# Seven block products for each pair of gate columns, with the convolution's norm moved into the attention slots

## The chip, the cores and the metric

The kernel runs on one core of a Trainium2 chip. The metric is the time of one execution in device microseconds, the median of several runs.

## What is computed

One encoder layer over 1024 positions of width 1024. What matters here is the first half, the mixing of positions:

```python
proj = x @ w_in[l] + b_in[l]
glu_in, q, k, v, gate_logits = jnp.split(proj, splits, axis=-1)     # 1024 | 512 | 512 | 512 | 2048 columns
y_conv = conv_branch(glu_in, ...)      # a * sigmoid(gate), 31 taps per channel, LayerNorm over 512 channels, SiLU, product
y_attn = chunked_attention(heads(q), heads(k), heads(v), rel_bias[l]) @ w_attn_out[l]
g_conv, g_attn = jnp.split(jax.nn.sigmoid(gate_logits), N_BRANCHES, axis=-1)
mixed = (g_conv * y_conv + g_attn * y_attn) @ w_o[l] + b_o[l]
x = layer_norm(ALPHA * x + mixed, ln1_g[l], ln1_b[l])
x = layer_norm(ALPHA * x + grouped_moe(x, ...), ln2_g[l], ln2_b[l])
```

Everything is float32. The expert half (16 experts, 2 used by each position) follows and is not touched, except for names of semaphores.

## The kernel before

Each product is made of float32r parts: ACT copies an operand into a rounded "high" tile, DVE (or POOL) subtracts it from the original into a "low" tile, and PE adds high x high, high x low and low x high (`mm3`, L544 to L546). A weight block is 128 columns of a weight matrix with all 1024 rows, 512 KB. SP loads block n into one of four ring slots once the slot's last block has been used (`wait_used`), ACT makes `wh` (L863), DVE makes `wl` (L1025).

A whole block is 8 row chunks x 2 halves of the sequence x 3 matmuls of 128x512, 48 in all. The order of PE is written by hand:

1. Blocks 0 to 7 are the convolution's input (values and gates). After each pair ACT takes the sigmoid and DVE makes `u` (`glu`, L1039).
2. Blocks 8 to 23 are the 16 gate blocks (`gate_job`). ACT writes their sigmoids to `gst`, and SP stores them to memory for later.
3. Meanwhile DVE does the convolution: 4 channel groups x 31 taps (`conv_tap`, L1052, first taps L1049), 7 taps per block. PE sums over channels with a matrix of ones (`conv_mean` before gate 14, `conv_var` before gate 15). DVE subtracts the mean (L1083), adds squares (L1066), takes one reciprocal of 128x1024 (L1089), and normalises (L1094); ACT applies SiLU (L920) while PE works on the first query and key blocks.
4. Eight tiles of v (128x256 matmuls), then the first query and key blocks in four half sums.
5. Attention in 32 slots (4 head pairs x 8 tiles of 128 queries). In slot n, PE makes the scores (L616), part of the next pair's query/key block, the weighted values of slot n-2 (L644) and the transposes of slot n-1 (L630). DVE takes the maxima of slot n (L1144), reciprocals (L1153), sums (L1163, L1168) and low parts of transposed tiles (L1175). ACT takes exponentials (L931), and POOL scales them (L499).

The DVE order in a slot before:

```python
for n in range(LATE):
    maxima(n)
    if n >= 2:
        transposed_lo(n - 2, now_and_late(n - 2)[1])
    inverse_sums(n)
    ...
    for p in qk_ended(n):
        qk_low(p, ps[:, qk_bank(p), :])
    if n >= 2:
        values_sum(n - 2)
    if n >= 1:
        transposed_lo(n - 1, now_and_late(n - 1)[0])
```

Of the kernel before, what the change touches and what calls it, by code (L numbers as in the profile page):

```python
# [13 lines left out]
P = 128  # L14
# [24 lines left out]
TAPS_A_STEP = 7  # L39
DMA_SCRATCH = 8192  # L40
# [5 lines left out]
B_GATE = 2 * CB  # L46
B_V = (24, 32)
B_Q = (26, 28, 30, 34)
B_OC, B_OA, B_WO = 36, 40, 44
N_BLOCKS = 52  # L50
LAST_GATES = (14, 15)


def block_columns():

    a, g, q, k, v, gate = 0, 4, 8, 12, 16, 20
    cols = []
# [26 lines left out]
def encoder_layer(nc, xT, x, wblk, b_in, dw, dwb, lncg, lncb, relb, b_o, ln1_g, ln1_b,  # L84
                  w_r, b_r, wexp, ln2_g, ln2_b, consts, out):
    x1_dram = nc.dram_tensor("x1_rows", (1 + SEQ, D), F32, kind="Internal").ap()
    acc_dram = nc.dram_tensor("acc_rows", (SEQ + P, D + 1), F32, kind="Internal").ap()
    gate_dram = nc.dram_tensor("gate_cols", (N_GATE, P, SEQ), F32, kind="Internal").ap()
    ctx = ExitStack()
    with ctx:  # L90
# [19 lines left out]
        csum = at("csum", [P, SEQ], F32, 112)  # L110
        sqr = at("sqr", [P, CB, SEQ], F32, 128)
# [83 lines left out]
        small = 211  # L195
# [24 lines left out]
        tab = tiny("tab", [P, 5, TAB], I32)  # L220
# [21 lines left out]
        par_in = sem("par_in"); bias_in = [sem(f"bias_in{i}") for i in range(2)]  # L242
# [7 lines left out]
        g_sig = sem("g_sig"); gs_out = [sem(f"gs_out{i}") for i in range(2)]  # L250
        mean_done = sem("mean_done"); cent = sem("cent"); sq_done = sem("sq_done"); sum_ok = sem("sum_ok")
        var_done = sem("var_done"); std_done = sem("std_done"); rstd_ok = sem("rstd_ok")
# [12 lines left out]
        row_in = [sem(f"row_in{i}") for i in range(TT)]  # L265
        lnp_in = sem("lnp_in"); xres_ok = sem("xres_ok")
# [5 lines left out]
        def wait_used(eng, n):  # L272

            if n < B_V[0]:
                eng.wait_ge(blk_used, n + 1)
            elif n in B_V or n - 1 in B_V:
# [9 lines left out]
        def place(n):  # L286

            if B_WO <= n < B_WO + 4:
                i = n - B_WO
                return wh2[:, i], wl2[:, i], raw2[:, i], raw2_in[i], 16  # L290
            s = n % RING
            return wh[:, s], wl[:, s], raw[:, s], raw_in[s], 16 * ((n if n < B_WO else n - 4) // RING + 1)

# [52 lines left out]
        SPLITS = {1: (30,), 2: (31,), 5: (32,), 9: (33,), 13: (34,), 17: (35,), 25: (36,), 27: (37,), 29: (38,), 30: (39,),  # L346
                  31: (40,), 32: (41,), 33: (42,)}
# [39 lines left out]
        def gate_q(g):  # L387

            return g if g < LAST_GATES[0] else 15 + 2 * (g - LAST_GATES[0])

        moe_parts = moe(nc, sem, locals())

        with nc.Block() as block:
            @block.sync
            def _(sp):
# [1810 lines left out]
```

## Time and profile before

| What | Value |
|---|---|
| median of 3 runs | 1134.77 us (1133.7 to 1134.91) |
| span of the profiled execution | 1130.7 us |
| median of the runs over that span | 4.07 us |
| busy: PE, DVE, ACT, POOL | 97%, 71%, 47%, 20% |
| chain that ended last, share of PE | 85% |
| mean granted TensorE clock | 0.991 |

The profile gives the span of its execution and not a separate device time for it; the 4.07 us between the span and the median of the runs is taken as what lies around a span. Busy shares are averages over stages. A matmul's listed duration overlaps the next one, so its rate is read from a window: time over count.

### The profile page before, as it was taken

To read this page: it belongs to the slowest core of one execution; us is meant where nothing else is said; L and a number is where in the kernel's file an instruction comes from. 1 tells how busy PE (TensorE), PEld (TensorE's weight loads), DVE (VectorE), ACT (ScalarE), POOL (GpSimd) and SP (SyncE) were. 2 spreads that over 40 slices of the span, in tenths; PEclk is the share of its full clock that TensorE was granted. 3 is DMA by queue.
4 is the path that set the end of the run, shared out by engine and by line. 5 is a ranking of instruction groups with operands and counts; after the bars stand their busy time and mean duration, and the time that the engine had idled before them with its cause. 6 is when DMAs were issued, how large, how long until landed. Compare 5 with 4: busy or idle time off the path is not lost.

```text
span 1130.7 us, 17012 instructions
## 1 busy us (share of the span) xinstructions
PE 1098.3 (97%) x5583; PEld 913.1 (81%) x5584; DVE 803.2 (71%) x1152; ACT 529.2 (47%) x787; POOL 227.4 (20%) x190
## 2 busy tenths in 40 slices
PE   8999999999999999999999999999999999999984
PEld 7888888888978789878888888787888888888762
DVE  5799999935447766666685588888679556558866
ACT  5111111123456665645331134467578545557755
POOL 0000000000046864757100000013121211212110
PEclk9999999999999999999999999999999999999998
DMA  7121233232111010181632325889999876699966
GB/s 266 56 84 56 83 104 104 83 112 93 57 38 43 19 43 1 65 326 39 251 118 88 142 119 196 278 331 354 324 331 381 311 230 192 236 352 341 368 177 269
DMA packets 49800, 199.58 MB, mean 177 GB/s; under 512 B 7249, under 2 KB 7633, under 8 KB 47682
## 3 DMA queue, kind: packets, MB, share of 16 engines
q1 hardware_dynamic: 43538, 176.19, 41.9%
q0 software_dynamic: 6192, 22.49, 8.0%
q8 instruction: 40, 0.66, 0.2%
q14 instruction: 30, 0.25, 0.1%
HBM read 166.21 MB, written 32.52 MB: 176 GB/s over the span
## 4 chain that ended last, share of the span: by engine, by line
PE 85%; DVE 4%; DMA 4%; ACT 3%; POOL 2%; issue 2%; ACTq 0%; DVEq 0%; SPq 0%; POOLq 0%
PE ps L544 16%; PE ps L546 16%; PE ps L545 16%; PE ps L1570 9%; PE ps L1572 9%; PE ps L1571 9%; PE ps L644 2%; PE ps L630 2%; DMA gu<-in_wexp 2%; PE ps L616 2%; DMA dn_raw<-in_wexp 2%; PE ps L1651 1%; PE ps L1566 1%; POOL pr L499 1%; PE ps L1678 1%
## 5 line engine op out<-in xcount | busy, mean ns | idle before, releaser
L544 PE MATMUL ps<-xh,wh 128*128 128x512 f32 x512 | 203.3, 397 | 2.0 <-DVE xl L1030 1.7
L545 PE MATMUL ps<-xl,wh 128*128 128x512 f32 x512 | 199.5, 390 | 0.0
L546 PE MATMUL ps<-xh,wl 128*128 128x512 f32 x512 | 199.5, 390 | 0.0
L1469 DVE TENSOR_TENSOR gu<-gu (+1 forms) x128 | 148.6, 1220 | 33.6 <-issue 21.5
L499 POOL TENSOR_SCALAR pr<-pr,rinv 128x640 f32<-128x640 f32 (+4 forms) x64 | 95.4, 1503 | 379.7 <-DVE rinv L1153 379.5
L1052 DVE SCALAR_TENSOR_TENSOR cv<-u,dw_t,cv 128x1024 f32<-128x1024 f32 x120 | 154.1, 1284 | 3.7
L1570 PE MATMUL ps<-gu,xgh 128*128 x336 | 134.0, 399 | 4.0 <-DVE gu L1469 2.2
L1463 ACT ACTIVATE gu<-gu (+1 forms) x128 | 124.4, 1048 | 20.6 <-DMA gu<-in_wexp 13.0
L1572 PE MATMUL ps<-gu,xgl 128*128 x336 | 131.9, 393 | 0.0
L1571 PE MATMUL ps<-gu,xgh 128*128 x336 | 131.4, 391 | 0.0
L544 PEld LDWEIGHTS ps<-xh,wh 128*128 128x128 f32 x512 | 96.1, 188 | 25.4 <-issue 6.4
L546 PEld LDWEIGHTS ps<-xh,wl 128*128 128x128 f32 x512 | 96.1, 188 | 20.5
L545 PEld LDWEIGHTS ps<-xl,wh 128*128 128x128 f32 x512 | 96.2, 188 | 19.1 <-issue 0.5
L863 ACT ACTIVATE wh<-raw 128x1024 fp32r<-128x1024 f32 x52 | 54.6, 1058 | 98.3 <-DMA raw<-in_wblk 98.0
L1025 DVE TENSOR_TENSOR wl<-raw,wh 128x1024 fp32r<-128x1024 f32 x40 | 50.3, 1260 | 47.7 <-ACT wh L863 47.5
L1570 PEld LDWEIGHTS ps<-gu,xgh 128*128 128x128 f32 x336 | 63.5, 189 | 17.9 <-issue 5.3
L2063 DVE TENSOR_TENSOR dn_l<-dn_raw,dn_h 128x1024 fp32r<-128x1024 f32 x60 | 69.5, 1220 | 9.9 <-ACT dn_h L1811 9.8
L1572 PEld LDWEIGHTS ps<-gu,xgl 128*128 128x128 f32 x336 | 63.4, 189 | 13.6
L1571 PEld LDWEIGHTS ps<-gu,xgh 128*128 128x128 f32 x336 | 63.6, 189 | 12.7
L1570 PE MATMUL ps<-dn_h,hbh 128*128 128x512 f32 x168 | 67.7, 403 | 2.5 <-DVE hbl L2067 2.5
L1572 PE MATMUL ps<-dn_h,hbl 128*128 128x512 f32 x168 | 66.3, 394 | 0.0
L1571 PE MATMUL ps<-dn_l,hbh 128*128 128x512 f32 x168 | 66.1, 394 | 0.0
(278 smaller groups left out, 2022.4 us busy)
## 6 DMA issues: line engine op xcount, KB each, us to landing
gu<-in_wexp SPq DMA_DIRECT2D x64, 1024.0 KB, 9.1
dn_raw<-in_wexp SPq DMA_DIRECT2D x16, 2048.0 KB, 9.8
raw<-in_wblk SPq DMA_DIRECT2D x52, 512.0 KB, 4.2
gate_cols<-gst SPq DMA_DIRECT2D x16, 512.0 KB, 5.3
xf<-acc_rows SPq DMA_DIRECT2D x8, 512.5 KB, 8.1
xraw<-in_xT SPq DMA_DIRECT2D x8, 512.0 KB, 7.3
gcm<-gate_cols SPq DMA_DIRECT2D x8, 512.0 KB, 7.5
gam<-gate_cols SPq DMA_DIRECT2D x8, 512.0 KB, 14.5
```

The lines of the kernel that those rows point to most:

```text
L499: pool.tensor_scalar(pr[n % 3][:, h, 0:nt * P], pr[n % 3][:, h, 0:nt * P], rinv[:, n % 3, h:h + 1], None, ALU.mult).then_inc(p_ready, 1)
L544: pe.matmul(o, a_h, b_h, start=first, stop=False)
L545: pe.matmul(o, a_h, b_l, start=False, stop=False)
L546: return pe.matmul(o, a_l, b_h, start=False, stop=last)
L863: act.activation(hi, src, ACT.Copy).then_inc(w_hi, 1)
L1052: dve.scalar_tensor_tensor(out=cv[:, j, :], in0=tap, scalar=w, in1=cv[:, j, :], op0=ALU.mult, op1=ALU.add).then_inc(conv_d, 1)
L1463: eng.activation(gu[:, par, k, 0, :], gu[:, par, k, 1, :].bitcast(F32), ACT.Copy).then_inc(gu_hi, 1)
L1469: eng.tensor_tensor(gu[:, par, k, 1, :], gu[:, par, k, 1, :].bitcast(F32), gu[:, par, k, 0, :], ALU.subtract).then_inc(gu_lo, 1)
L1570: pe.matmul(o, a_h, b_h, start=first, stop=False)
L1571: pe.matmul(o, a_h, b_l, start=False, stop=False)
L1572: return pe.matmul(o, a_l, b_h, start=False, stop=last)
L2063: dve.tensor_tensor(dn_l[:, k, :], dn_raw[:, k, :], dn_h[:, k, :], ALU.subtract).then_inc(dn_lo, 1)
```

## The change

The 16 gate blocks form 8 pairs. For a pair, the product of a 2x2 grid of weight parts (2 blocks x 2 halves of the rows) with a 2x2 grid of input parts (2 halves of the rows x 2 halves of the sequence) was 8 block products. It becomes 7, in the scheme with 4 sums of weights, 4 sums of inputs and 7 sums of results. A block product ("unit") is 4 chunks x 3 = 12 matmuls of 128x512, and there are 56.

- POOL makes the weight sums with DMAs from memory to memory: per pair 4 copies and 4 adding transfers of 256 KB, issued in 7 rounds of up to 16, each round waiting for all of the one before.
- SP loads 56 units of 256 KB into 8 slots, in place of 16 blocks. A summed unit waits for its round.
- DVE makes the four input sums (128x2048 each) and their low parts; ACT makes the high parts.
- For each unit ACT makes a high part, DVE a low part (128x512); DVE adds results (7 additions per pair), ACT copies one product and takes four sigmoids per pair.
- Each block of the first eight still has 7 taps beside it (from the third on), but in the gate stage one tap goes with each unit. Sixteen more stand beside the v tiles and ten behind them.
- The mean's matmuls stand between the third and fourth query/key half sums, the centring behind them; squares, variance, square root, reciprocal, normalisation and SiLU stand in attention slots 0 to 9.
- The two first bias tiles are scaled by POOL instead of DVE.
- v tiles use other PSUM banks, and the query/key sums wait for all eight low parts of v.

The core of the diff. Of the two functions named `conv_late` the first is ACT's, called ahead of a slot's exponentials, and the second DVE's, called between `maxima(n)` and the rest of slot n:

```diff
+UNIT_SLOTS = 8
+PARTS = {1: (0, 0), 2: (0, 1), 4: (1, 1)}
+SUMS = {5: 0, 6: 1, 7: 2, 3: 3}
+ORDER = (1, 6, 5, 7, 2, 3, 4)
+UNITS = [(x, q) for q in range(KC) for x in ORDER]
...
+                            if stage:
+                                pool.dma_start(o, a, accum_op=ALU.add, max_dma_last_dim=4096).then_inc(wsum_in, 16)
+                            else:
+                                pool.dma_start(o, a).then_inc(wsum_in, 16)
+                for r in range(KC // 2 + 3):
+                    if r:
+                        pool.wait_ge(wsum_in, 16 * sums_issued(r - 1))
+                    for stage in range(4):
+                        weight_sums(r - stage, stage)
...
+                def gate_product(m):
+                    x, q = UNITS[m]
+                    s, bank = m % UNIT_SLOTS, m % 8
+                    pe.wait_ge(u_lo, m + 1)
+                    if m < 8:
+                        pe.wait_ge(u_ready, CB - 1 + (m >= 4))
+                    else:
+                        bank_read(m - 8)
...
+                    for k in range(CB):
+                        last = mm3(ps[:, bank, :], uh[:, s, k], ul[:, s, k], b_h[:, k, :], b_l[:, k, :],
+                                   k == 0, k == CB - 1)
+                    last.then_inc(blk_used, 1)
...
-                    v_tile(0, t, ps[:, 4 + t % 4, 0:2 * P])
+                    v_tile(0, t, ps[:, V_BANKS[t % 4], 0:2 * P])
+                pe.wait_ge(v_lo, TT)
                 for i in range(2):
...
+                        if i and h == 0:
+                            conv_mean()
...
                 for n in range(LATE):
                     scores_of_slot(n)
+                    if n == VAR_SLOT:
+                        conv_var()
...
+                def conv_late(n):
+                    if n == 1:
+                        act.wait_ge(stat_done, 2)
+                        act.activation(std[:], psf[:, 6 * HALF:8 * HALF], ACT.Sqrt, scale=1.0 / DC, bias=eps[:]).then_inc(sq_done, 1)
+                    if n == SILU_SLOT:
+                        for j in range(CB):
+                            act.wait_ge(nrm, j + 5)
+                            act.activation(cv[:, j, :], cv[:, j, :], ACT.Silu, scale=cpar[:, 1, j:j + 1],
...
+                for m in range(N_UNITS):
+                    if m + 4 < N_UNITS:
+                        unit_low(m + 4)
+                    if m == 0:
+                        glu(CB - 1)
+                    if m:
+                        gate_sums(m - 1)
+                    some_taps(TAPS_A_PRODUCT)
...
                 for t in range(TT):
+                    some_taps(2)
+                    v_low(0, t, ps[:, V_BANKS[t % 4], 0:2 * P])
...
+                some_taps(CB * CW)
...
+                def conv_late(n):
+                    if n == 0:
+                        for j in range(1, CB):
+                            square_sum(j)
+                    if n in (2, 3):
+                        dve.wait_ge(sq_done, CB + 1)
+                        for i in range(2 * n - 4, 2 * n - 2):
+                            c = slice(2 * P * i, 2 * P * i + 2 * P)
+                            dve.reciprocal(rstdc[:, c], std[:, c]).then_inc(nrm, 1)
+                    if 4 <= n < 4 + CB:
+                        normalise(n - 4)
```

Three places in the instruction order, all on DVE. In the names, `cv` is the convolution's sum, `ul` and `uh` a unit's low and high part, `gst` the gate results, `vhl` the parts of v, `pr` the attention tile and `nmx` its maxima.

The gate stage before, in its middle:

```order
L1052 SCALAR_TENSOR_TENSOR cv<-u,dw_t,cv 128x1024 x7
L1025 TENSOR_TENSOR wl<-raw,wh 128x1024
L1052 SCALAR_TENSOR_TENSOR cv<-u,dw_t,cv 128x1024 x7
L1025 TENSOR_TENSOR wl<-raw,wh 128x1024
L1052 SCALAR_TENSOR_TENSOR cv<-u,dw_t,cv 128x1024 x7
```

And now:

```order
L1230 TENSOR_TENSOR ul<-uraw,uh 128x512
L1256 TENSOR_TENSOR gst<-ps,gst 128x512
L1212 SCALAR_TENSOR_TENSOR cv<-u,dw_t,cv 128x1024
L1230 TENSOR_TENSOR ul<-uraw,uh 128x512
L1212 SCALAR_TENSOR_TENSOR cv<-u,dw_t,cv 128x1024
L1230 TENSOR_TENSOR ul<-uraw,uh 128x512
L1256 TENSOR_TENSOR gst<-ps,gst 128x512
```

Seven taps and one 128x1024 subtraction per block of 48 matmuls became one tap, one 128x512 subtraction and on average one addition from PSUM per unit of 12.

The v stage before ends like this:

```order
L1099 TENSOR_TENSOR vhl<-ps,vhl 128x2x128 x4
L1113 TENSOR_SCALAR bias_75<-bias_75 128x1280
L1115 MEMSET bias_75 64x2x64
L1116 MEMSET bias_75 64x2x64
L1113 TENSOR_SCALAR bias_76<-bias_76 128x1280
L1115 MEMSET bias_76 64x2x64
```

And now, up to the first maxima:

```order
L1212 SCALAR_TENSOR_TENSOR cv<-u,dw_t,cv 128x1024 x2
L1324 TENSOR_TENSOR vhl<-ps,vhl 128x2x128
L1212 SCALAR_TENSOR_TENSOR cv<-u,dw_t,cv 128x1024 x2
L1324 TENSOR_TENSOR vhl<-ps,vhl 128x2x128
L1212 SCALAR_TENSOR_TENSOR cv<-u,dw_t,cv 128x1024 x10
L1220 TENSOR_TENSOR csum<-csum,cv 128x1024
L1332 SCALAR_TENSOR_TENSOR ql_77<-ps,b_in_t,qh_75 128x512 x2
L1348 SCALAR_TENSOR_TENSOR cv<-ps,cv 128x1024 x4
L1332 SCALAR_TENSOR_TENSOR kl_81<-ps,b_in_t,kh_79 128x512 x2
L1185 TENSOR_TENSOR wl<-raw,wh 128x1024 x2
L1384 ISA pr_86,nmx<-ps,bias_84 128x128
```

Taps stand ahead of each low part of v, and the last taps, the channel sum and the centring stand ahead of the key's low parts, which the first scores need.

Attention slot 2 on DVE before:

```order
L1144 ISA pr_79,nmx<-ps,bias_75 128x384
L1144 ISA nmx 128x1
L1153 RECIPROCAL rinv<-rs 128x1 x2
L1163 TENSOR_TENSOR attn<-ps,attn 64x128 x2
L1168 TENSOR_TENSOR attn<-ps,attn 64x128 x2
```

And now:

```order
L1384 ISA pr_88,nmx<-ps,bias_84 128x384
L1384 ISA nmx 128x1
L1364 RECIPROCAL rstdc<-std 128x256 x2
L1393 RECIPROCAL rinv<-rs 128x1 x2
L1403 TENSOR_TENSOR attn<-ps,attn 64x128 x2
L1408 TENSOR_TENSOR attn<-ps,attn 64x128 x2
L1415 TENSOR_TENSOR pthl<-ps,pthl 128x4x128
```

Half of the reciprocal over 1024 positions stands between the slot's maxima and everything else that PE waits for; slot 3 has the other half. Over the whole program PE's list shrinks from 5412 to 5316 rows.

## Rows read from the trace of the kernel before

**Rows 1.** Busy time by stretch, us: engine busy (instructions), granted clock, DMA share, GB/s.

```profile
core 0: us, PE busy (x) PEld busy (x) DVE busy (x) ACT busy (x) POOL busy (x), PEclk, DMA share, GB/s
95.80:247.80 152.00, 152.00 (x672) 125.88 (x671) 128.73 (x103) 30.26 (x28) 0.00 (x0) 1.00 0.30 90
272.94:295.97 23.03, 23.03 (x194) 23.03 (x192) 10.83 (x13) 4.75 (x9) 0.00 (x0) 1.00 0.22 70
295.97:317.85 21.88, 21.88 (x99) 17.85 (x98) 7.17 (x12) 10.16 (x11) 0.00 (x0) 1.00 0.22 72
317.85:339.93 22.08, 22.08 (x129) 17.52 (x128) 12.90 (x45) 15.10 (x35) 14.09 (x11) 1.00 0.17 48
339.93:364.65 24.72, 24.30 (x167) 20.78 (x166) 18.45 (x54) 16.75 (x40) 17.86 (x11) 1.00 0.15 49
```

**Rows 2.** Waits of PE up to 520 us: total, times, longest us.

```profile
PE ps L544 <- DVE xl L1030: 1.7, 1, 1.7
PE ps L630 <- POOL pr L499: 1.4, 2, 0.8
```

**Rows 3.** Groups of DVE up to 330 us: busy us, mean ns | idle before.

```profile
L1052 DVE SCALAR_TENSOR_TENSOR cv<-u,dw_t,cv 128x1024 f32<-128x1024 f32 x120 | 154.1, 1284 | 3.7
L1025 DVE TENSOR_TENSOR wl<-raw,wh 128x1024 fp32r<-128x1024 f32 x30 | 36.6, 1224 | 44.8 <-ACT wh L863 44.6
L1089 DVE RECIPROCAL rstdc<-std 128x1024 f32<-128x1024 f32 x1 | 6.6, 6553 | 1.2 <-ACT std L891 1.2
L1039 DVE SCALAR_TENSOR_TENSOR u<-ps,b_in_t,sig 128x1024 f32<-128x1024 f32 x4 | 5.1, 1278 | 0.0
L1066 DVE TENSOR_TENSOR sqr<-sqr 128x1024 f32<-128x1024 f32 x3 | 3.7, 1225 | 1.2 <-ACT sqr L888 1.0
L1099 DVE TENSOR_TENSOR vhl<-ps,vhl 128x256 fp32r<-128x256 f32 x8 | 3.4, 425 | 12.8 <-ACT vhl L903 12.8
```

**Rows 4.** Timeline of DVE, first blocks: start, duration us.

```profile
21.00 1.23 DVE L1025 TENSOR_TENSOR wl<-raw,wh 128x1024 fp32r<-128x1024 f32 x1 [0.24 <-ACT wh L863]
38.02 7.89 DVE L1052 SCALAR_TENSOR_TENSOR cv<-u,dw_t,cv 128x1024 f32<-128x1024 f32 x6
46.96 9.21 DVE L1052 SCALAR_TENSOR_TENSOR cv<-u,dw_t,cv 128x1024 f32<-128x1024 f32 x7
```

**Rows 5.** Timeline of PE: first product, mean, scores of slots 0 and 5, values in slot 9.

```profile
8.16 0.47 PE L544 MATMUL ps<-xh,wh 128*128 128x512 f32 x1 [1.71 <-DVE xl L1030]
247.64 1.88 PE L583 MATMUL ps<-csum,ones_c 128*128 128x512 f32 x4
317.85 0.33 PE L616 MATMUL ps<-kh,qh 64*128 64x128 f32 x2
339.93 0.41 PE L616 MATMUL ps<-kh,qh 64*128 64x320 f32 x2
368.83 1.36 PE L644 MATMUL ps<-pthl,vhl 128*128 128x256 f32 x10
```

**Rows 6.** Timeline of ACT at a table load, and the group of SiLUs.

```profile
296.17 0.38 ACT L903 ACTIVATE vhl<-ps 128x256 fp32r<-128x256 f32 x1 [2.50 <-PE ps L546]
296.57 1.28 ACT L920 ACT_TABLE_LOAD   x1
...
L920 ACT ACTIVATE cv<-cv,cpar 128x1024 f32<-128x1024 f32 x4 | 4.6, 1231 | 0.0
```

**Rows 7.** The first 15 us, columns as in rows 1.

```profile
0.00:15.00 15.00, 11.55 (x44) 9.32 (x46) 9.13 (x9) 10.13 (x11) 1.73 (x12) 1.00 0.88 345
```

**Rows 8.** POOL DMA issues, ns min/median/max; landing; packets of one scatter (791.6 to 803).

```profile
L1507 POOL DMA_INDIRECT acc_rows<-ys,to_now x20: 1591/1607/2427, 755.5 to 1089.7; - x20
...
L1497 POOL DMA_INDIRECT xg<-x_rows,id_now x19: 965/1006/1187, 731.2 to 1052.3; - x19
...
acc_rows<-ys,to_now POOLq DMA_INDIRECT x20, 9.3
...
q0 software_dynamic: 144, 0.52, 29.7%
```

More of the change, by code:

```diff
@@ L289, in place, with gate_weights, sum_round, sums_issued @@
                 i = n - B_WO
-                return wh2[:, i], wl2[:, i], raw2[:, i], raw2_in[i], 16
+                return wh2[:, i], wl2[:, i], raw2[:, i], raw2_in[i], 48 if i < 2 else 16
             s = n % RING
             return wh[:, s], wl[:, s], raw[:, s], raw_in[s], 16 * ((n if n < B_WO else n - 4) // RING + 1)
+        def gate_weights(q, n, k):
+            return wblk[W_GATE + 2 * q + n][:, CB * k:CB * k + CB, :]
+        def sum_round(x, q):
+            return q // 2 + {5: 1, 7: 1, 6: 2, 3: 3}[x]
+        def sums_issued(r):
+            return sum(2 * many for g in range(KC // 2) for stage, many in enumerate((4, 2, 1, 1)) if g + stage <= r)
+        U2, W, U3, C22, C11, C12, C21 = range(1, 8)
+        def sum_no(which, q):
+            return 7 * q + which
+        def sigmoids_at(m):
+            if not 0 <= m - 2 < N_UNITS:
+                return []
+            x, q = UNITS[m - 2]
+            return [(q, slot) for after, slot in ((7, 3), (2, 0), (3, 2), (4, 1)) if after == x]
+        SIGMOIDS = [x for m in range(N_UNITS + 2) for x in sigmoids_at(m)]
+        def sigmoid_no(q, slot):
+            return SIGMOIDS.index((q, slot)) + 1
+        V_BANKS = (0, 1, 2, 3)
         def tiles_of(c):
@@ L593, in v_part @@
+                    last.then_inc(stat_done, 1)
                 def v_part(s, t, o, ks):
@@ new lines, in _ @@
+                    if n == 0:
+                        for i in range(4):
+                            act.wait_ge(t_sum, i + 1)
+                            act.activation(t_high[i], t_raw[i], ACT.Copy).then_inc(x_hi, 1)
+                    j = n // 2
+                    if n % 2:
+                        act.wait_ge(blk_used, n + 1)
+                        if j >= 2:
+                            act.wait_ge(u_ready, j - 1)
+                        g = 4 * (j % 2) + 2
+                        act.activation(sig[:, j % 2, :], psf[:, HALF * g:HALF * g + SEQ], ACT.Sigmoid,
+                                       bias=b_in_t[:, CB + j:CB + j + 1]).then_inc(sig_ready, 1)
@@ L899, in v_high @@
+                for m in range(N_UNITS + 2):
+                    if m < N_UNITS:
+                        copy_product(m)
+                    if m + 4 < N_UNITS:
+                        unit_high(m + 4)
+                    elif m + 4 < N_UNITS + 2:
+                        high(B_V[0] + m + 4 - N_UNITS)
+                    for q, slot in sigmoids_at(m):
+                        gate_sigmoid(q, slot)
                 def v_high(s, t, o):
@@ L952, in _ @@
                 for i in range(2):
-                    act.wait_ge(gs_out[i], 16 * KC)
+                    for slot in range(4):
+                        act.wait_ge(row_moved[4 * i + slot], GATES_STORED)
                 def conv_high(n):
@@ new lines, in _ @@
+                assert taps == CB * CW
+                for i in range(2):
+                    qk_low(i, ps[:, i, :])
+                dve.wait_ge(stat_done, 1)
+                for j in range(CB):
+                    dve.scalar_tensor_tensor(out=cv[:, j, :], in0=psf[:, 4 * HALF:6 * HALF], scalar=-1.0 / DC, in1=cv[:, j, :],
+                                             op0=ALU.mult, op1=ALU.add).then_inc(cent, 1)
+                for i in range(2, 4):
+                    qk_low(i, ps[:, i, :])
@@ L1131, in maxima @@
+                for i in range(2):
+                    for slot in range(4):
+                        dve.wait_ge(row_moved[4 * i + slot], GATES_STORED)
                 def maxima(n):
```

425 lines of the change are left out of this document (254 added, 171 removed).

## The prediction

> **What bounds the kernel now.** I read busy time by stretch first. In the gate stage PE is busy in all of 152.0 us, for 672 matmuls, so one costs 152.0 / 672 = 0.226 us; a block of 48 takes 10.86 us and a unit of 12 will take 2.71 us. The granted clock is 1.00 there and in the stretches after it [rows 1]. PE's waits come next: in the first 520 us the longest are 1.7 us at the start and 1.4 us for POOL [rows 2]. So each matmul taken out before the experts is worth its full time, and each wait put in costs its full time, since nothing later on PE is idle enough to win it back. The reader should then look at DVE in the same stretches: 128.7 of 152.0, 10.8 of 23.0, 7.2 of 21.9, 12.9 of 22.1 and 18.5 of 24.7 us [rows 1]. That idle time must hold all that the change adds to DVE.
>
> **What is taken away.** PE's list has 96 rows fewer, all of them gate matmuls: 96 x 0.226 = **21.7 us**. The four matmuls of the mean (1.88 us with their overlap, about 1.7 in the queue [rows 5]) and the four of the variance are only moved.
>
> **What is put on the path.** Durations of DVE for sizes that the trace lacks come from the line through 256 columns (425 ns) and 1024 columns (1224 ns) [rows 3]: 0.69 us for 512 and 2.3 for 2048.
>
> (a) *Start.* POOL's first round copies 8 x 256 KB = 2.1 MB from about 2 us on, beside the loads of x, whose stretch runs at 345 GB/s [rows 7]; PE is paced by them, for it waits for the first low part of x and then has 0.6 us of slack. If none of it gets in the way this costs 0, if all goes first 2.1 MB / 345 GB/s = 6.1 us. I take 2, a third, since the copies are issued one by one, a plain one in about 1.0 us of POOL [rows 8].
>
> (b) *Unit 4 waits for `glu(3)`.* DVE is free at 22.2 us [rows 4]. It makes the four input sums (4 x 2.3, to 31.4), a `wl` behind ACT's rounded parts of them (to 35.6) and their four low parts (to 44.4). Then 6 x 7 taps at 9.2 us for seven [rows 4] less the two cheap first taps make 54.3, three `wl` 3.4, five unit low parts 3.1 and four `glu` 4.8 (1.2 each, back to back) [rows 3]: 110.0 us. PE could start unit 4 at 95.8 + 4 x 2.71 = 106.7. Cost 3.3; between 1 and 6, for 88 us of queue are added up. From there DVE needs about 17.5 us per seven units (7 x 0.6 low parts, 7 x 0.66 additions, 7 x 1.25 taps) against PE's 19.0, so it keeps ahead, with ACT at under half. This cover is thin: 0.2 us more per unit would use it up.
>
> (c) *v to query/key.* Between the last unit and the eighth low part of v, DVE has one addition 0.7, 16 taps 20.5, eight low parts 3.4 and two `wl` 2.4 [rows 3]: 27.0, or 26.7 with their overlap, against 23.0 us of PE [rows 1]. PE now waits for all eight: 3.7 (3 to 5).
>
> (d) *The way to the first scores.* From the start of the query/key sums (time 0) DVE has ten taps, the channel sum and two low parts, to 15.8. The mean's matmuls run from 16.3 to 18.0, the four centrings to 22.9; ACT squares the last until 24.1 and only then takes the key's high part (24.8), DVE its low part (25.5). Scores start at 25.6 where they stood at 21.9 [rows 1]; 1.7 of that is the mean. Cost 2.0 (1 to 4).
>
> (e) *Slots 0 to 4.* PE waits, followed in the queues: 1.3 for a `wl` that now stands behind (d); 2.5 for three square additions of 1.2 [rows 3] ahead of the variance; 0.8 because ACT loads the square root's table, takes the root and loads the exponential's table ahead of slot 1's exponentials; 2.1 and 3.5 for the two halves of the reciprocal, 3.3 us each (6.55 in one piece [rows 3]), which stand ahead of the inverse sums, the low parts and the next maxima. That is 10.2, of which 0.6 comes back: 9.6. Lower bound 5: DVE is busy 12.9 of 22.1 us there, so has 9.2 idle for 10.3 of new work [rows 1]. Upper 12.
>
> (f) *Slots 4 to 7*, one normalisation of 1.2 each against 6.3 us idle [rows 1]: 1.5 (0 to 4).
>
> (g) *SiLU in slot 9.* Ahead of that slot's exponentials ACT now has a table load, four SiLUs (4.6) and the load back: 1.28 + 4.6 + 1.28 = 7.2 us [rows 6]. The late transposed tile of slot 7 is queued behind it, and the weighted values, at 368.8 before [rows 5], wait for that tile. ACT had some 1.6 us idle there: 5.5 (2 to 7).
>
> Nothing else is charged: scaling two bias tiles on POOL (3.5 us each) lies in the 20 us before the first maxima, and everything behind slot 9 keeps its order.
>
> **Sum.** 2 + 3.3 + 3.7 + 2.0 + 9.6 + 1.5 + 5.5 = 27.6 put in, 21.7 taken out: **+5.9 us** on a span of 1130.7. The median of the runs is 4.07 above that span, so 1134.77 + 5.9 = **1140.7**. With all terms at their low ends (12) the result is -9.7, with all at the high ends (44) +22.
>
> A rule weighed against a row. A table load stands 0.02 us behind the operation before it and takes 1.28 us, after which SiLU starts at once [rows 6]. The Trainium skill (ScalarE: Activation LUTs, What ACT_TABLE_LOAD costs) adds a drain of 1.38 us to each switch. The row shows none, and decides; with it, four more switches in the slots would add up to 5.5 us and the time would be 1146.
>
> **Rivals.**
>
> *B, faster: the slots absorb it.* PE's queue in each early slot holds a filler of 12 matmuls (2.7 us), placed so that the chain from maxima to transposes has time; if the queues overlap better than I follow them, (e) and (g) shrink. With (a) at 0, (b) 2, (c) 3, (d) 1, (e) 5, (f) 0 and (g) 2 the sum is 13, and the time 1134.77 - 8.7 = 1126. It decides as soon as (e) and (g) together are under 6.9 us instead of 15.1. For it: PE waits almost nowhere today. Against: DVE's added 10.3 us in slots 0 to 3 exceed its idle time. Chance 0.27.
>
> *C, a draw*, within 2.3 us of the time before (0.2%, about what a measurement of this kernel can tell from no change): (e) and (g) near 9. Chance 0.15.
>
> *D, the weight sums come late.* Unit 5 is the first to need the fourth round, so 8 + 12 + 14 + 16 = 50 transfers with four landings between. With 32 copies at 1.0 us, 18 adding ones at 1.6 and 9.3 us to land [rows 8] that is 2 + 32 + 29 + 37 = 100 us, and the data is needed by about 106. At the longest issues seen, 1.19 and 2.43 us [rows 8], it is 121, which is 15 late: 1155; with all 50 at 2.43, 160 and about 1190. SP's queue waits in order, so later loads are late with it. Later rounds have slack: 144 packets of one scatter, 0.52 MB, took 29.7% of 11.4 us of the 16 engines, or 3.4 us [rows 8], and 32 such transfers of half the size need 54 us of some 200. Chance 0.11. The Trainium skill (SBUF — State Buffer, SBUF: two separate sides) says that POOL cannot write descriptors while DVE holds their shared port in its fast mode; by that, POOL's issues would stretch beside a busy DVE, and this rival is how it would show. No row shows the rule at work on plain transfers.
>
> That the change does not do what it says is excluded by PE's list.
>
> **How the numbers follow.** Forecast 0.47 at 1140.7, B 0.27, C 0.15, D 0.11. Faster by over 0.2%: 0.27; within: 0.15; slower: 0.47 + 0.11 = 0.58. The likeliest case's own range is 1137 to 1152. The range 1123 to 1160 leaves out about half of D and the thin ends of B and of the forecast.
>
> **What would show it.** Right: 56 units at 2.71 us; a wait of PE of about 3 us for `u` or `ul` near 107 us; about 4 us for `vhl` before the query/key sums, near 276; waits for `sqr` and for DVE's reciprocals in slots 1 to 4; a wait of about 5 us near 370 behind ACT's SiLU. Wrong: PE at over 99% through slots 0 to 9 (B), waits for unit loads behind POOL's rounds (D), or a unit stage longer than 160 us, which would mean that DVE's additions are dearer than 0.66 us.

## The result and the profile after

| | before | changed |
|---|---|---|
| median, us | 1134.24 (1132.82 to 1134.91, 4 runs) | 1159.8 (1155.37 to 1160.31, 4 runs) |
| ratio | 1 | 1.0217, 95% interval 1.0196 to 1.0238 |
| profiled execution: own time, span, us | 1134.77, 1130.7 | 1159.61, 1157.8 |
| granted clock, mean | 0.991 | 0.975 |

Slower was right, the size was not: +25.6 us where +5.9 was forecast. The time lies at the upper edge of the whole range (1123 to 1160) and above the likeliest case's own (1137 to 1152). The busy table of the changed kernel, cut where PE starts the first product, the first unit, the v tiles, the query/key sums and the scores of slots 0, 5, 9 and 11 (the columns are those of [rows 1]):

```profile
8.01:100.79 92.78, 88.64 (x385) 71.71 (x386) 76.99 (x57) 28.18 (x26) 32.33 (x50) 1.00 0.86 238
100.79:262.89 162.10, 154.87 (x673) 127.45 (x672) 150.99 (x181) 56.75 (x93) 7.16 (x9) 0.98 0.56 157
262.89:296.19 33.30, 23.45 (x194) 23.04 (x192) 33.02 (x31) 8.86 (x15) 8.01 (x6) 0.92 0.35 119
296.19:324.00 27.81, 26.13 (x102) 20.36 (x102) 20.67 (x19) 6.78 (x8) 0.00 (x0) 0.91 0.10 24
324.00:356.89 32.89, 28.51 (x132) 21.36 (x132) 25.59 (x56) 18.36 (x38) 14.57 (x11) 0.84 0.09 29
356.89:382.72 25.83, 24.29 (x167) 20.75 (x166) 22.03 (x56) 16.34 (x38) 17.35 (x11) 1.00 0.13 47
382.72:400.39 17.67, 12.45 (x57) 9.89 (x56) 7.14 (x25) 14.18 (x24) 6.80 (x6) 0.81 0.00 1
```

And the stretch of before that answers to the last line:

```profile
364.65:374.32 9.67, 9.37 (x58) 7.66 (x57) 7.01 (x24) 6.72 (x17) 3.59 (x3) 1.00 0.00 1
```

Against [rows 1] this gives the ledger of the span. The first unit starts 5.0 us later (100.79 for 95.80). The units take 162.1 us; 672 matmuls took 152.0 before, so 10.1 are lost there. The v tiles lose 10.3 (33.3 for 23.0). The query/key sums lose 4.2 beside the 1.7 of the moved mean, slots 0 to 4 lose 9.1 beside the 1.7 of the moved variance, slots 5 to 8 1.1, the stretch of slot 9 8.0, all the rest 1.0. That is 48.8 put in and 21.7 taken out: +27.1, the difference of the spans (1157.8 - 1130.7). PE's waits up to 420 us name the causes (the line left out is 1.7 us for POOL's `zeros` at the start, which the kernel before has too):

```profile
PE ps L651 <- DVE vhl L1324: 9.8, 2, 9.4
PE ps L769 <- DVE pthl L1415: 6.4, 3, 4.5
PE ps L651 <- DVE u L1199: 5.9, 1, 5.9
PE ps L651 <- DVE xl L1190: 4.1, 5, 1.2
PE ps L651 <- DVE ql L1332: 3.5, 2, 2.7
...
PE ps L741 <- DVE kl L1332: 1.7, 1, 1.7
PE ps L651 <- DVE ul L1230: 1.4, 1, 1.4
PE ps L651 <- DVE wl L1185: 1.2, 1, 1.2
```

These are 34 us, where [rows 2] had nothing over 1.7, and all eight are waits for DVE. They are not the whole loss. Five times PE's granted clock stands at a half (of its two levels, 1.2 GHz instead of 2.4) behind a wait. The same columns for these five stretches:

```profile
119.35:122.90 3.55, 3.55 (x9) 2.78 (x9) 3.55 (x5) 0.00 (x0) 0.35 (x1) 0.50 0.58 113
296.19:300.62 4.43, 4.43 (x10) 3.46 (x11) 4.32 (x4) 0.00 (x0) 0.00 (x0) 0.50 0.00 0
325.78:330.64 4.86, 4.86 (x11) 3.81 (x12) 4.65 (x8) 3.44 (x6) 0.00 (x0) 0.50 0.00 0
352.28:354.37 2.09, 2.09 (x6) 1.60 (x5) 2.09 (x7) 0.71 (x1) 0.89 (x1) 0.51 0.00 0
393.95:398.78 4.83, 4.83 (x12) 3.77 (x12) 2.63 (x11) 2.59 (x6) 3.90 (x3) 0.50 0.01 3
```

In them one matmul follows another after 0.427 us instead of 0.227, so 19.8 us of them cost about 19.8 x (1 - 0.227 / 0.427) = 9.3 us. This is an estimate and the least: right behind the five stretches another 4.7 us run at 0.51 to 0.53, which by the same sum would be 2.2 us more. The kernel before has a granted clock of 1.00 in each of the stretches of [rows 1].

### The profile page after: what moved, and what is told of

Its sections match the earlier page's. It is cut to its first block, busy times and chain, and to the rows that moved or that the text cites. A ratio compares the mean times of both kernels' runs of the same rounds, so it can differ in the third digit from the quotient of the medians.

```text
span 1157.8 us, 17221 instructions
## 1 busy us (share of the span) xinstructions
PE 1094.1 (94%) x5487; PEld 905.0 (78%) x5488; DVE 866.4 (75%) x1253; ACT 560.2 (48%) x856; POOL 282.5 (24%) x259
## 4 chain that ended last, share of the span: by engine, by line
PE 58%; DVE 10%; ACT 4%; DMA 4%; issue 2%; POOL 1%; ACTq 0%; DVEq 0%; SPq 0%; POOLq 0%
PE ps L1810 9%; PE ps L1812 9%; PE ps L1811 9%; PE ps L651 7%; PE ps L652 7%; PE ps L653 7%; DVE cv L1212 2%; PE ps L769 2%; DMA gu<-in_wexp 2%; DMA dn_raw<-in_wexp 2%; PE ps L755 1%; PE ps L1891 1%; PE ps L741 1%; PE ps L1806 1%; ACT pr L1089 1%
## 5 line engine op out<-in xcount | busy, mean ns | idle before, releaser
L1703 ACT ACTIVATE gu<-gu (+1 forms) x128 | 124.0, 1048 | 22.2 <-DMA gu<-in_wexp 13.9
L651 PE MATMUL ps<-xh,wh 128*128 128x512 f32 x256 | 107.6, 420 | 18.3 <-DVE vhl L1324 9.4
L652 PE MATMUL ps<-xl,wh 128*128 128x512 f32 x256 | 103.3, 404 | 0.0
L653 PE MATMUL ps<-xh,wl 128*128 128x512 f32 x256 | 103.0, 402 | 0.0
L651 PEld LDWEIGHTS ps<-xh,wh 128*128 128x128 f32 x256 | 49.8, 195 | 34.9 <-DVE vhl L1324 9.6
L1089 ACT ACTIVATE pr<-pr,nmx 128x640 f32<-128x640 f32 (+4 forms) x64 | 44.1, 690 | 45.7 <-DVE nmx L1384 45.7
L2051 ACT ACTIVATE dn_h<-dn_raw 128x1024 fp32r<-128x1024 f32 x60 | 58.7, 1048 | 8.2 <-DMA dn_raw<-in_wexp 4.6
L1415 DVE TENSOR_TENSOR pthl<-ps,pthl 128x512 fp32r<-128x512 f32 (+1 forms) x72 | 41.1, 598 | 26.1 <-ACT pthl L1106 25.4
L1747 POOL DMA_INDIRECT acc_rows<-ys,to_now x20 | 36.9, 1843 | 94.9 <-ACT ys L2076 85.0
```

Source lines behind the costliest of these rows:

```text
L651: pe.matmul(o, a_h, b_h, start=first, stop=False)
L652: pe.matmul(o, a_h, b_l, start=False, stop=False)
L653: return pe.matmul(o, a_l, b_h, start=False, stop=last)
L1703: eng.activation(gu[:, par, k, 0, :], gu[:, par, k, 1, :].bitcast(F32), ACT.Copy).then_inc(gu_hi, 1)
L2051: act.activation(dn_h[:, k, :], dn_raw[:, k, :], ACT.Copy).then_inc(dn_hi, 1)
```

## The experiments

All are compared with the kernel before on the same chip, whose median there was 1133.2 to 1134.3 us. "Less than the changed kernel" is measured from the 1159.8 above (1155.4 to 1160.3), so a difference of 5 us or less rests on the stretches of the profile and not on the times. Theory T1: separate stalls that add up, each from a queue that was full or out of order at its place, and behind each stall a price in clock.

**1. No weight sums.**

```
- (POOL) for r in range(KC // 2 + 3): ... weight_sums(r - stage, stage)
- (SP, load_unit) sp.wait_ge(wsum_in, ...)
+ (SP, load_unit) source is always a plain block of gate weights
```

> The changed kernel without POOL's weight sums: no copies and no additions from memory to memory, every unit loads a plain weight block (so four of seven block products of each group are computed from the wrong weights; the arithmetic of every engine is the same). Theory T1 (the sums' copies crowd the loads of the first 30 us): the first product comes about 5 us earlier (the first unit near 96 us instead of 100.8), the third weight low part ends near 22 us instead of 31, glu(3) ends near 109 instead of 118, the wait of unit 4 for u falls from 5.9 us to under 2.5, and its half-clock stretch goes; in all 9 to 16 us less than the changed kernel, 1144 to 1151. Rival (the DVE chain is late because the units' own low parts and the input sums are put on it, whatever the DMA engines do): 5 us less from the start alone, the wait for u stays at 4 us or more, 1154 to 1156. Rival (the sums' traffic costs throughout, also in units 10 to 55): the unit stage from unit 8 on gets shorter per unit by over 1%.

Measured: 1164.0 us in all, which says nothing, because wrong gates send other numbers of tokens to the experts (the part behind slot 11 took 772 us for 757, with 84 matmuls more). Up to the scores of slot 11 it is 389.5 us against 400.4. The first unit starts at 95.2, the wait for `u` is 3.3, the unit stage 157.5 us. So the sums cost 5.6 us at the start and 4.6 in the units, and 5.5 of the units' loss is still there without them: both T1 and its first rival hold a part. The second rival falls: from unit 8 on nothing is left to win (experiment 7 reaches 152.3 us for the units with the sums in place).

**2. The sums start later.**

```
+                pool.wait_ge(w_hi, 4)
                 for r in range(KC // 2 + 3):
```

> The changed kernel with its weight sums started later: POOL waits for the fourth weight block's high part (about 21 to 26 us) before the first copies. T1: start and DVE chain as without any sums (first unit near 96 us, wait for u under 2.5 us), but the four rounds that unit 5 needs end 15 to 20 us later than now (they ended near 96 us), near 110, which is the time at which unit 5 is wanted; so 8 to 13 us less than the changed kernel where that still fits (1147 to 1152), or a new wait of PE of 3 to 8 us for unit 5's low part that eats half of it (1152 to 1156). Rival (the DVE chain is late by itself): 1154 or more with the wait for u as before.

Measured: **1150.1** (1148.5 to 1152.3), 9.7 less than the changed kernel. The timeline of DVE in the changed kernel shows what the copies did to the weight blocks behind x:

```profile
25.73 1.23 DVE L1185 TENSOR_TENSOR wl<-raw,wh 128x1024 fp32r<-128x1024 f32 x1 [1.44 <-ACT wh L983]
30.87 1.23 DVE L1185 TENSOR_TENSOR wl<-raw,wh 128x1024 fp32r<-128x1024 f32 x1 [3.92 <-ACT wh L983]
32.01 2.28 DVE L1234 TENSOR_TENSOR t_raw<-xraw 128x2048 f32<-128x2048 f32 x1
```

and the same three operations with the sums started later:

```profile
19.29 1.23 DVE L1186 TENSOR_TENSOR wl<-raw,wh 128x1024 fp32r<-128x1024 f32 x1 [0.96 <-ACT wh L984]
20.78 1.23 DVE L1186 TENSOR_TENSOR wl<-raw,wh 128x1024 fp32r<-128x1024 f32 x1 [0.26 <-ACT wh L984]
21.92 2.28 DVE L1235 TENSOR_TENSOR t_raw<-xraw 128x2048 f32<-128x2048 f32 x1
```

The input sums start at 21.9 instead of 32.0, which is what the prediction had assumed (22.2). The first unit starts at 95.3; PE waits 2.9 us for `u` instead of 5.9 and no longer for `ul`. The feared wait of unit 5 for the fourth round did not come.

**3. Bias tiles scaled on ACT.**

```
- (POOL, scale_bias) pool.tensor_scalar(t[:], t[:], 1.0 / SCALE, None, ALU.mult)
+ (ACT, tile 0 behind v_high(5), tile 1 behind qk_high(1))
+                    act.activation(bias[b][:], bias[b][:], ACT.Copy, scale=1.0 / SCALE)
```

> The changed kernel with the multiplications of bias tiles 0 and 1 moved from POOL to ACT (tile 0 behind the sixth value tile's high part, tile 1 behind the first two query and key high parts). T1 (a POOL operation over SBUF holds up DVE operations with two SBUF operands): the low part that took 3.74 us and the two taps that took 5.01 us return to about 1.2 and 2.6, the wait of PE for vhl falls from 9.8 us to about 5, and the half-clock stretch behind it gets shorter; 4 to 8 us less, 1152 to 1156. Rival (those operations were slow by chance or through DMA writes into SBUF): the same two stay slow, 0 to 1 us, 1158 to 1160.

Measured: **1155.0** (1150.5 to 1157.4), 4.8 less. POOL in the changed kernel:

```profile
271.40 3.46 POOL L597 TENSOR_SCALAR bias<-bias 128x1280 f32<-128x1280 f32 x1 [143.26 <-DMA bias<-in_relb]
...
277.58 3.75 POOL L597 TENSOR_SCALAR bias<-bias 128x1280 f32<-128x1280 f32 x1 [2.20 <-DMA bias<-in_relb]
```

and DVE at the same time:

```profile
271.77 3.74 DVE L1185 TENSOR_TENSOR wl<-raw,wh 128x1024 fp32r<-128x1024 f32 x1
275.43 2.59 DVE L1212 SCALAR_TENSOR_TENSOR cv<-u,dw_t,cv 128x1024 f32<-128x1024 f32 x2
277.94 0.42 DVE L1324 TENSOR_TENSOR vhl<-ps,vhl 128x256 fp32r<-128x256 f32 x1
278.27 5.01 DVE L1212 SCALAR_TENSOR_TENSOR cv<-u,dw_t,cv 128x1024 f32<-128x1024 f32 x2
283.20 0.42 DVE L1324 TENSOR_TENSOR vhl<-ps,vhl 128x256 fp32r<-128x256 f32 x1
283.53 1.22 DVE L1185 TENSOR_TENSOR wl<-raw,wh 128x1024 fp32r<-128x1024 f32 x1
```

A weight block's low part takes 3.74 us under POOL's operation and 1.22 without, two taps take 5.01 and 2.59: 4.9 us. In the kernel before DVE did the two scalings itself in 0.82 us each, so 1.6 us of DVE were saved for 4.9. Both read two operands from SBUF. The value's low part at 277.94, which reads PSUM and one operand from SBUF, keeps its 0.42 us although POOL is at work. With the scaling on ACT (1.27 us each) all low parts of blocks take 1.22 and all pairs of taps 2.60. The Trainium skill (SBUF — State Buffer, Who interferes with whom) states this rule: a DVE instruction with two SBUF inputs and a GpSimd instruction that reads SBUF exclude each other. The trace agrees; the held low part ends 0.65 us behind POOL's operation.

```profile
262.26:290.63 28.37, 23.19 (x193) 22.99 (x192) 28.08 (x31) 9.12 (x16) 0.40 (x2) 1.00 0.40 139
```

This is the v stage then: 28.4 us for 33.3, with DVE busy in 28.1 of them. DVE's own queue, not POOL, is what is left.

**4. No SiLU.**

```
-                            act.activation(cv[:, j, :], cv[:, j, :], ACT.Silu, scale=..., bias=...)
+                            act.activation(cv[:, j, 0:1], cv[:, j, 0:1], ACT.Copy)
```

> The changed kernel without the four SiLU operations in slot 9 (a one-column copy stands in their place, so the convolution branch lacks its activation), and with them without the two table loads around them. Theory: slots 9 to 11 take 9.7 to 10.5 us instead of 17.7 (this prices term (g), foretold 5.5 us, measured as 8.0 with a stretch at half clock in it): 7 to 8.5 us less than the changed kernel, 1151 to 1153. Rival (the 8 us are mostly the delay of DVE, carried along from slots 4 to 8, and show later anyway): under 5 us.

Measured: 1214.6 in all, again of no use (the part behind slot 11 took 821 us with other routing and 336 matmuls more), but the stretch itself is clear:

```profile
381.60:391.27 9.67, 9.34 (x57) 7.63 (x57) 7.04 (x24) 7.23 (x21) 3.61 (x3) 1.00 0.01 2
```

9.67 us, to the hundredth as before, for 17.67. Term (g) is 8.0, not 5.5, with its share of half clock in it.

**5. SiLU in slot 18.**

```
- VAR_SLOT, SILU_SLOT = 1, 9
+ VAR_SLOT, SILU_SLOT = 1, 18
```

> The changed kernel with SiLU in slot 18 instead of slot 9. Theory (SiLU and its two table loads keep ACT from the transposed probabilities for 7.2 us, which costs 8.0 us in slot 9 where PE has little else, and less where PE has twice the work of its own): slots 9 to 11 take 9.7 us instead of 17.7, slot 18 and the one behind it grow by 1 to 4 us: 4 to 7 us less, 1153 to 1156. Rival (ACT's 7.2 us are on the path in any slot, since each slot's chain scores, maxima, exponentials, transposes runs through ACT): under 1.5 us, 1158 or more.

Measured: **1159.5** (1158.0 to 1161.2): nothing gained. The theory fell and the rival held. Slots 17 and 18, and 19, of this run:

```profile
425.60:444.44 18.84, 13.32 (x94) 11.55 (x94) 7.48 (x26) 14.50 (x25) 6.82 (x6) 0.93 0.00 0
444.44:454.23 9.79, 9.79 (x54) 8.03 (x54) 3.92 (x12) 3.50 (x10) 6.84 (x5) 0.78 0.01 2
```

and of the kernel before:

```profile
409.87:422.43 12.56, 12.34 (x93) 11.09 (x92) 7.20 (x25) 7.02 (x18) 6.40 (x5) 1.00 0.01 2
422.43:430.30 7.87, 7.87 (x55) 6.76 (x54) 4.12 (x13) 3.90 (x11) 7.25 (x6) 1.00 0.00 0
```

6.3 + 1.9 = 8.2 us, as in slot 9, again with half clock in it. That ACT is busy in 7.0 of 12.6 us does not mean that a block of 7.2 fits: the longest idle piece of ACT in these 12.6 us was 1.55 us, and PE now waits 5.3 us for the low part of a value tile, whose high part stands behind the block in ACT's queue.

**6. PE kept busy through a wait.**

```
+                pe.wait_ge(c_sum, sum_no(C21, KC - 1))
+                for i in range(38):
+                    pe.matmul(ps[:, 4, :], xh[:, i % KC, 0:P], xh[:, i % KC, 0:HALF], start=True, stop=True)
                 pe.wait_ge(v_lo, TT)
```

> The changed kernel with 38 matmuls of 128x512 that nobody reads behind the last value tile, so that PE is busy for 8.6 us of the 9.4 us that it waits for vhl there (nothing else is changed). Theory (the half clock of 290.4 to 300.7 us comes from PE standing still, and costs about 2.2 us of the query and key products behind the wait): the wait ends at the same time, the granted clock stays at 1.0 there and the query and key products take 25 to 26 us instead of 27.8: 2 to 2.5 us less, 1157.0 to 1158.0. Rival (the clock falls because of heat or power of all engines, not because PE stood still): the same half clock, or more of it; 0, or slower by the fillers.

Measured: **1155.8** (1153.5 to 1158.6), 4.0 less than the changed kernel by doing more. The v stage and the query/key stage:

```profile
262.49:296.10 33.61, 32.09 (x232) 30.04 (x230) 33.33 (x31) 8.86 (x15) 8.86 (x6) 1.00 0.36 117
296.10:321.62 25.52, 23.85 (x102) 18.70 (x102) 20.68 (x19) 6.78 (x8) 0.00 (x0) 1.00 0.09 26
```

The wait ends at the same time (296.10 for 296.19), the clock stays at 1.00, and query/key takes 25.5 us instead of 27.8. The half-clock stretch of slot 0 went too, though the waits of 1.7 and 1.2 us ahead of it are still there, and slots 0 to 4 took 0.8 us less; up to slot 5 that is 3.1 us. The profiled executions differ by 1.0 us in all (1156.8 for 1157.8) and the times overlap, so the 3.1 us of these stretches are the measure and not the 4.0. So the half clock behind the long wait follows from PE standing still; why that of slot 0 went is open. In this run POOL's scaling started earlier and met two pairs of taps (5.23 and 5.21 us) and no low part of a block: it stops what happens to be there.

**7. Combinations.** Four edits at first (2, 3, SiLU in 18, the reciprocal in quarters in slots 2 to 5); then the taps dealt out anew:

```
-                        some_taps(TAPS_A_STEP)
+                        some_taps(3 if n == B_V[0] - 1 else TAPS_A_STEP)
-                    some_taps(TAPS_A_PRODUCT)
+                    some_taps(2 if m % 6 == 3 and m > 6 else TAPS_A_PRODUCT)
```

> Four edits on the changed kernel together: weight sums started behind the fourth block's high part (measured alone: 9.7 us less), bias tiles 0 and 1 scaled on ACT (measured alone: 4.8 us less), SiLU in slot 18 instead of 9, and the reciprocal of the standard deviation a quarter in each of slots 2 to 5 with the normalisation in slots 6 to 9. Theory T1 (the losses are separate stalls that add up): 14.5 us less from the first two, 4 to 7 us from the third, 0 to 2 us from the fourth: 1136 to 1141 us. Rival (the losses hide one another, DVE's backlog being one and the same): under 16 us in all, 1144 or more.

> The version with the four edits, and DVE's taps dealt out anew: 3 instead of 7 in the last step before the units (so glu(3) comes 5 us earlier), two instead of one behind units 9, 15 and so on to 51, so that 22 instead of 26 are left for the value stage. T1 (unit 4 waits for glu(3), and the value stage is as long as DVE's queue in it): against the version with four edits the wait for u (2.9 us) and the half clock behind it (about 2 us) go, and the value stage gets 3 to 5 us shorter: 6 to 10 us less, 1128 to 1134 us. Rival (DVE is full in the unit stage, so every tap moved there delays the units' own low parts): the same time as the version with four edits, within 2 us, with PE waiting for ul or for sums instead.

Measured: **1143.3** (1139.6 to 1149.9) and **1141.3** (1137.2 to 1142.3). The first is 2 us above its expectation, which had counted 4 to 7 us for SiLU in slot 18, where experiment 5 found nothing to win. The second (1128 to 1134 expected) falls short in the time and holds in one place: PE's wait for `u` is gone. Its unit stage is without loss, its v stage is not better than in experiment 3:

```profile
95.22:247.54 152.32, 152.32 (x673) 126.13 (x672) 151.05 (x180) 56.45 (x92) 11.35 (x14) 1.00 0.61 171
247.54:276.44 28.90, 23.19 (x193) 22.98 (x191) 28.62 (x32) 10.14 (x16) 0.40 (x2) 0.98 0.40 137
```

152.3 us is the forecast's 56 x 2.71, with DVE busy in 151.1 of it and the weight sums running. The four taps saved came off the end of DVE's list, behind the eight low parts for which PE waits.

**8. Queues put in order.** One tap instead of two ahead of each of v's low parts, reciprocals in slots 10, 11, 13 and 15, normalisation in 16 to 19, one SiLU in each of slots 18 to 21:

> The version with four edits and the taps dealt out anew, with three edits more: one tap instead of two ahead of each value tile's low part (the eight left over come behind the last one, where DVE stood idle for 10 us in two gaps), the four quarters of the reciprocal in slots 10, 11, 13 and 15 with the normalisation in slots 16 to 19, and the four SiLU operations one by one in slots 18 to 21, each with its own two table loads. Theory T1 (PE waits where DVE's or ACT's queue is full, and each engine has room elsewhere): the wait of PE for vhl in the value stage (5.7 us) goes and with it the half clock behind it (1 to 2 us), slots 2 to 8 are as in the kernel before (4 to 5 us less than with the reciprocals in slots 2 to 9), and SiLU costs 0 to 4 us in place of 8.2, since each slot from 17 on has 3.5 to 4.4 us in which ACT does nothing and one SiLU with its loads takes 3.7: 14 to 19 us less than that version's 1141, 1122 to 1128, which is under the kernel before (1134). Rival (ACT is in the chain of each slot, so that its work costs its full length wherever it stands): SiLU now costs up to 15 us, 1134 to 1140.

Measured: **1130.4** (1126.7 to 1135.3), ratio 0.9976 (0.9949 to 1.0003), 11 us less than the version before it, where 14 to 19 were expected. The v stage takes 24.1 us; slots 2 to 8 are as before the change. PE now waits 3.1 us for the channel sum, ahead of which the eight taps stand. Slots 17 to 21 take 43.0 us for 37.7 before, so one SiLU per slot, with the normalisation beside it, costs 5.3 us where the block in slot 18 cost 8.2. ACT's timeline of the kernel before shows a reason, ahead of a slot's first exponential:

```profile
433.73 0.83 ACT L931 ACTIVATE pr<-pr,nmx 128x640 f32<-128x640 f32 x1 [2.24 <-DVE nmx L1144]
```

and this run's shows filled:

```profile
425.53 1.28 ACT L1093 ACT_TABLE_LOAD   x1
426.83 1.24 ACT L1093 ACTIVATE cv<-cv,cpar 128x1024 f32<-128x1024 f32 x1
428.09 1.28 ACT L1100 ACT_TABLE_LOAD   x1
429.39 0.83 ACT L1100 ACTIVATE pr<-pr,nmx 128x640 f32<-128x640 f32 x1
```

3.8 us go into a gap of 2.2, and that slot takes 9.4 instead of 8.5 us.

**9. Three orders more, and SiLU in a block.**

```
- (DVE) for t in range(TT): some_taps(1)
+ (DVE) for t in range(TT): some_taps(2 if t in (3, 5, 6, 7) else 1)
- (DVE) qk_low(0), qk_low(1), centring, qk_low(2), qk_low(3), low(B_Q[1]), low(B_Q[1] + 1)
+ (DVE) qk_low(0), qk_low(1), qk_low(2), low(B_Q[1]), low(B_Q[1] + 1), centring, qk_low(3)
- (ACT) four squares, qk_high(2), qk_high(3)
+ (ACT) qk_high(2), three squares, qk_high(3), the last square
```

> The version with all edits, and three places put in another order: four of the eight taps come back ahead of the value low parts where DVE waited for ACT (so the column sum is ready 5 us earlier), the third query and key part and the low parts of two weight blocks come ahead of the mean on DVE (where it stood idle), and ACT makes the fourth key part ahead of the last square. Theory T1: the waits for csum (3.1 us), for kl (1.7, to under 1), for wl in slot 0 (1.2) and the half clock behind them (about 1.5) go: 5 to 7.5 us less than that version's 1130.4, 1123 to 1126, faster than the kernel before by 0.7 to 1.0%. Rival (the same waits come back at the next place that needs DVE, the second maxima): 1128 to 1130.

> The reordered version, but with the four SiLU operations together in slot 20 between one pair of table loads. Theory (ACT stands idle for 2.0 to 2.2 us ahead of the first exponential of each slot of that part, and only what is longer than that gap delays the slot: 4 single ones with loads of 3.8 us delay by 1.6 each, the block of 7.2 us by 5): the block costs 5 to 8 us against 4.6 to 6.4 for the four: the same within 2 us, with the delay in one slot and a stretch at half clock behind it. Rival (each table load costs more than its own 1.28 us): the block is faster by 3 us or more.

Measured: **1126.1** (1125.6 to 1126.7), ratio **0.9926** (0.9908 to 0.9944), faster than the kernel before; and 1125.7 (1121.7 to 1128.6) with the block of SiLUs in slot 20, the same. The waits for `csum`, `kl` and the `wl` of slot 0 are gone, and query/key takes 23.8 us. In the time the block is no dearer than four single ones, but that hides two differences. Slots 17 to 21 take 44.7 us with the block and 42.0 with the four (37.7 before), so the block costs 7.0 us there and the four 4.4. Slot 1, which is the same program in both, took 8.3 us with the block and 10.0 with the four, since behind the same wait of 2.8 us for `sqr` the clock stayed full in one execution and not in the other (first the version with the block, then the one with four):

```profile
302.67:307.61 4.94, 4.87 (x18) 3.21 (x18) 0.73 (x5) 2.85 (x4) 1.20 (x2) 1.00 0.00 0
302.70:309.21 6.51, 6.51 (x19) 3.73 (x19) 0.62 (x4) 2.83 (x4) 1.20 (x2) 0.74 0.00 0
```

So the price in clock of a wait of this length is not the same each time.

**10. The root behind the exponentials.**

```
- (ACT, slot 1) root, exponential 0, exponential 1
+ (ACT, slot 1) exponential 0, exponential 1, root
```

> The reordered version, with ACT's square root of slot 1 behind that slot's two exponentials instead of ahead of them (the same number of table loads). In the reordered version slot 1 takes 10.0 us against 3.76 in the kernel before, because the exponentials stand behind the root, the root behind the variance's matmuls, and those behind DVE's three additions of squares. Theory T1 (the order in ACT's queue chains PE's transposes to the variance): the transposes of slot 1 come 3 to 5 us earlier, slots 0 to 4 take 24 to 26 us instead of 28.3: 1.5 to 4.5 us less, 1122 to 1124.5. Rival (the next exponentials and the query part wait for the root instead): within 1 us of 1126.

Measured: 1124.7 (1123.0 to 1129.1), within 1.4 us of the four-SiLU version of experiment 9; the time alone lies between the two expectations. The span up to slot 5 is the same (324.0 for 324.2), and slot 1 still takes

```profile
299.07:309.05 9.98, 7.16 (x26) 4.34 (x26) 4.22 (x11) 5.16 (x12) 3.00 (x4) 0.83 0.00 0
```

The rival held: PE's own queue has the variance (2.8 us of wait for DVE's three additions of squares, then its matmuls) and twelve matmuls of the query ahead of the transposes, so ACT's order did not matter.

## Why the prediction was right and wrong

The gain was exact: 96 matmuls fewer, and once nothing stalls a unit stage of 152.3 us. The direction followed from a right reading of where DVE and ACT fill up. That 1159.8 falls inside 1123 to 1160 is luck: the top of that range stood for rival D, which did not happen, and all terms at their high ends gave +22. Terms (b), (c), (d) and (g) came out above their own bounds. One reading was loose and changed nothing: the 1.4 us for POOL in [rows 2] are two waits, the longest 0.8. Of the seven terms:

- **(a)** 2, measured 5.0 to 5.6 (experiments 1, 2). "A third" of 6.1 was taken because the copies are issued one by one; they were issued at 4.39 us for eight, 0.55 each and not 1.0, and PE lost nearly the whole of the 6.1.
- **(b)** 3.3. "DVE is free at 22.2 us" is the step that failed: the same copies delayed the weight blocks, and DVE reached its input sums at 32.0. Where that is mended the wait is 2.9 us (3.3 without any sums): the queue itself was added up rightly. Even so the units take 158.2 us there, since half clock comes on top.
- **(c)** 3.7. The added-up queue was 1.7 too short (10.3 less the 4.9 of POOL is 5.4, as in experiment 3). The larger miss is the sentence "nothing else is charged: scaling two bias tiles on POOL": it stopped DVE for 4.9 us, because only POOL's time was looked at and not what shares its way to SBUF.
- **(d)** 2.0: with full clock query/key takes 25.5 us, less the mean 1.7 and the 21.9 of before, which is 1.9. Right.
- **(e)** 9.6 for 9.1 in all, but 3.3 of these are clock ((4.86 + 2.09) x 0.468), so the waits were at most 5.9: the sum was right by chance, and PE's queue hid more of DVE's work than I followed. The reciprocal is the larger part: with it in slots 10 to 15 (experiment 8) slots 0 to 4 take 27.0 us, which leaves 3.2 of the 9.1. **(f)** 1.5 for 1.1: right.
- **(g)** 5.5, measured 8.0 in slot 9 and 8.2 in slot 18. In slot 9 the clock took about 2.3 (4.83 x 0.468); without it 5.7 are left, so the wait itself was sized rightly.
- **The step that failed in four of them**, (b), (d), (e) and (g), and the largest: "each wait put in costs its full time". It costs more. PE's clock stood at a half behind five of the waits, at least 9.3 us in all by the estimate above; of this experiment 6 shows the part of (d), 2.3 us. With the clock counted by itself the miss of 21.2 us on the span (27.1 - 5.9) divides into clock 9.3, POOL's hold on DVE 4.9, (b) 5.1 (10.1 less 1.7 of clock, less 3.3), (a) 3.0, (c) 1.7, all behind slot 11 1.0, (g) and (d) 0.3, less 3.7 for (e) and 0.4 for (f). It adds up by construction: what the clock does not take stays with its term.

Rival D did not happen: the fourth round was done at about 96 us, since issues took half of what was assumed (0.55 us for a plain one, 0.86 for the adding ones from the weights, where 1.0 and 1.6 were taken). The rule of the Trainium skill that was named with it (SBUF — State Buffer, SBUF: two separate sides: POOL cannot write descriptors while DVE holds the shared port in its fast mode) does not show on plain transfers here: eight plain issues take 4.1 to 4.4 us in each of the first four rounds, the fourth in a stretch in which DVE is busy in 4.06 of 4.17 us, though with operations that read two operands from SBUF. Whether it shows elsewhere is open: in the middle of the fourth round POOL stands idle for 9.0 to 11.4 us in each run with the sums, with nothing to wait for in the profile and DVE at its taps. The table load of slot 9 shows no drain either; it starts 0.01 us behind the tile copy, lasts 1.28, and SiLU starts 0.02 us behind it. Rivals B and C fell with (e) and (g).

What stays open: the last two versions win 8 of the 21.7 us. Of the rest about 4.5 lie in slot 1 (9.98 us, less the variance's 1.7, for 3.76 before; where the clock stayed full the slot took 8.3) and about 5 in slots 15 to 21, where the normalisation and SiLU are; that they can't be hidden was not shown. One part is known: in the last version a normalisation takes 2.78 us for 1.22, because POOL makes the low part of a weight block (2.40 us) at the same time, as in experiment 3. How the 9.1 us of (e) divide among squares, square root and reciprocal no run shows beyond the above.

## What to carry to other kernels

Where PE has no idle time, price a new wait at its length plus what the half clock behind it may cost, and look for the wait's cure in the order of the queue that is late: here the same arithmetic, dealt out in another order, turned 2.2% slower into 0.7% faster. Count every engine's queue up to the operation that is waited for and not to the end of the stage, since work taken off behind it wins nothing. Before work is moved to POOL or to its DMA queue as if free, ask what DVE reads at that time and which loads the first microseconds need.

## What the runs showed of the hardware

- PE's granted clock stood at a half behind waits of 2.7 to 9.4 us, once behind two of 1.7 and 1.2 us close together, for 2 to 6 us of matmuls; filling 8.8 us of such a wait with matmuls that nobody reads kept it at full and made query/key 2.3 us shorter. Not each such wait does it: behind the same 2.8 us the clock was 1.00 in one execution and 0.74 in another.
- A POOL operation over SBUF stops DVE operations with two SBUF operands (3.74 for 1.22 us; two taps 5.01 for 2.59) and not one that reads PSUM and SBUF (0.42 for 0.42).
- ACT scales a tile of 128x1280 in 1.27 us, DVE in 0.82, POOL (beside a busy DVE) in 3.46 to 3.75.
- Eight plain copies of 256 KB on POOL's queue were issued in 4.39 us and took a share of the DMA engines from loads issued at the same time by SP: `x` landed after 10.7 us (median) instead of 7.3.
